# Twelve modulation weight blocks split four and eight, and relative-bias tables read from a skewed copy

## The chip, the cores and the metric

The kernel runs on one core of a Trainium2 chip. The metric is device time in microseconds (us) of one execution. A core has five engines that run their own instruction streams and meet through semaphores: TensorE (PE, with weight loads shown as PEld), VectorE (DVE), ScalarE (ACT), GpSimd (POOL) and SyncE (SP). SP issues the large weight loads, POOL the small and indirect ones. In this profile TensorE's granted clock is given as a share of its higher level: 1.0 is 2.4 GHz, 0.5 is 1.2 GHz.

## The reference

Two blocks of two layers each work on a sequence of 512 tokens of width 1024. The change touches only the first block, which for each layer does this:

```python
mod = c_act @ w_ada[l] + b_ada[l]                 # 1024 x 6144 weights, one row of input
sh1, sc1, g1, sh2, sc2, g2 = jnp.split(mod, 6, axis=-1)
h = modulate(rms_norm(x, norm1_g[l]), sh1, sc1)   # needs sh1, sc1 alone
y = token_mixer(h, ...)                           # gated linear attention and differential attention
x = x + g1[:, None, :] * y                        # needs g1
h = modulate(rms_norm(x, norm2_g[l]), sh2, sc2)   # needs sh2, sc2
y = hier_moe(h, ...)
x = x + g2[:, None, :] * y                        # needs g2
```

In the differential attention a bias is added to the scores of 4 heads. It depends on key position minus query position alone: `bucket = t5_bucket(kpos - qpos)`, `bias = rel_bias[bucket]`, 32 buckets by 4 heads. Each head makes two softmaxes p0 and p1 and uses `p0 - lam * p1` on the values.

## The kernel before, in words

Activations are held transposed: 8 tiles of 128 features by 512 tokens. Weights pass through a ring of six slots (`ring`, 2 MB each); a block is 1024 x 512 numbers of float32. The list `blocks_a` gives the blocks in the order in which SP loads them, each with its slot and the last ticket that reads it. SP walks this list in order: for each block it waits until the reader before it in that slot is done, then issues the load (line 569). `order_a` lists the tickets: each is one output of TensorE in one of the eight PSUM banks, in the order in which TensorE makes them. The consumer (`"V"` for DVE, `"A"` for ACT) frees the bank.

Modulation. `w_ada` of a layer is twelve blocks, named `("ada", j)`. For each, TensorE does 32 matmuls of 128 columns (8 row groups by 4 column groups, two records each in the trace) into one bank. DVE adds the twelve results one after another into `T[:, 0]` (lines 1414 and 1417). After the twelfth, TensorE turns that tile (`("adt",)`, line 935), DVE adds the bias into `mod` (line 1421) and makes the scales `s1` of both norms. `mod_ready` then lets ACT scale and shift the first norm's output (line 1935), after which the first projection, `("lr",)`, can start. Blocks 0 to 5 take slots 0 to 5, blocks 6 to 11 the same slots again. Blocks 0 to 3 hold sh1 and sc1; blocks 4 and 5 g1; 6 to 9 sh2 and sc2; 10 and 11 g2.

The first norm runs beside it: ACT squares x (line 1926), TensorE sums the squares, DVE and ACT take the root and its reciprocal (lines 1400, 1930, 1402), and DVE multiplies eight tiles (line 1409). DVE does this ahead of all adds of the modulation.

Differential attention. A loop of 18 iterations i over 4 heads by 4 query tiles. TensorE makes two score tiles L(i) and turns the weights of step i-2, T(i-2) (line 1059). At the last query tile of a head it multiplies by the values, pv(h). DVE in iteration i waits for T(i-2), then adds the bias and takes the row maximum (line 1556), and forms the weights of step i-1 (lines 1564 to 1567). ACT takes the exponentials (line 2046) and copies T (line 1908). The bias table of a head, 128 rows by 896, lies in one of two tiles `relm`; POOL loads it (line 689) for heads 0 and 1 long before the loop and for heads 2 and 3 when the head two before is done.

Setup. POOL writes constants and loads `c`, the bucket table and the 32 x 4 bias values. TensorE makes a tile of 4 x 1024, one row per head, and DVE copies it; POOL stores it to `rel_scratch` and reads it back 128 times with a row step of one element, so that partition p holds the row moved by p. This lies in reversed partition order, and TensorE turns it round with a reversed identity (8 matmuls of 448 columns); DVE copies the result and POOL stores it to `relm_scratch`. SP starts the first weight load only after that read-back has landed (`rel_loaded`, line 518). DVE then clears two tiles and releases the first layer. POOL waits for its stores before it issues the thirteen parameter loads of the layer.

The line that makes SP wait, and the one that sets the slots:

```python
sp.wait_ge(rel_loaded, 16 * HEADS)
return [(name, last, n % RING if n < 12 else n % 3, None) for n, (name, last) in enumerate(b)]
```

Of the kernel before, what the change touches and what calls it, by code (L numbers as in the profile page):

```python
# [34 lines left out]
P = 128  # L35
# [24 lines left out]
REL_W = 896  # L60

SCRATCH = 6144

LINKS = {"A": 176, "B": 138}
# [76 lines left out]

def order_a():
    t = [(("n1",), "V")] + [(("ada", j), "V") for j in range(12)] + [(("par",), "V"), (("adt",), "V"), (("lr",), "A")]
# [30 lines left out]
    t += [(("on", h), "V") for h in range(HEADS)]  # L174
# [16 lines left out]
def blocks_a():  # L191

    b = [(("ada", j), ("ada", j)) for j in range(12)]
    b += [(("lr",), ("lr",)), (("gqk",), ("gq", 1)), (("gv",), ("gv", 3)), (("gg",), ("gg", 3)), (("dq",), ("dq", 3)),
          (("dk",), ("dk", 3)), (("dv",), ("dv", 3))]
    for j in range(2):
        b += [((w, j), (w, 4 * j + 3)) for w in ("ga", "ya", "gb", "yb")]
    b += [(("wo", 0), ("wo", 3)), (("wo", 1), ("wo", 7)), (("rt",), ("rt",))]

    return [(name, last, n % RING if n < 12 else n % 3, None) for n, (name, last) in enumerate(b)]  # L200
# [77 lines left out]
def program(nc, ctx, inp, out):  # L278
# [52 lines left out]
    rel_dram = nc.dram_tensor("rel_scratch", [HEADS, 1024], F32).ap()  # L331
    relm_dram = nc.dram_tensor("relm_scratch", [HEADS, P, REL_W], F32).ap()
# [87 lines left out]
    rel_stored, rel_loaded = sem("rel_stored"), sem("rel_loaded")  # L420
# [81 lines left out]
    def tok(t, n=1):  # L502
        return slice(t * P, (t + n) * P)
# [5 lines left out]
    def _(sp):  # L509
# [6 lines left out]
        sp.wait_ge(started, 1)  # L516

        sp.wait_ge(rel_loaded, 16 * HEADS)
# [95 lines left out]
    def _(pool):  # L614
# [6 lines left out]

        did(pool.memset(ident[:], 0.0))
# [4 lines left out]
        did(pool.memset(T[:, 1, 0:P], 0.0))  # L627
        did(pool.affine_select(out=T[:, 1, 0:P], in_=T[:, 1, 0:P], compare_op=ALU.not_equal, fill=1.0, base=-(P - 1), pattern=[[1, P]], channel_multiplier=1))
        did(pool.iota(cells[:], pattern=[[0, 2]], base=0, channel_multiplier=0))
        pool.dma_start(prow[0:KD, 0, :], inp["c"][0].rearrange("(k p) -> k p", p=P)).then_inc(setup_d, 16)  # L630
        pool.dma_start(flat(U[0:BUCKETS, 0:2]), inp["buckets"]).then_inc(setup_d, 16)
        pool.dma_start(U[0:BUCKETS, 2, 0:HEADS], inp["rel_bias"]).then_inc(setup_d, 16)
# [38 lines left out]
        pool.wait_ge(setup_v, 1)  # L671
        pool.dma_start(rel_dram, flat(U[0:HEADS, 4:6])).then_inc(rel_stored, 16)
        pool.wait_ge(rel_stored, 16)
        for h in range(HEADS):
            row = rel_dram[h:h + 1, 0:REL_W]
            src = bass.AP(tensor=row.tensor, offset=row.offset, ap=[[1, P], [1, REL_W]])
            pool.dma_start(flat(U[:, 8 + 2 * h:10 + 2 * h])[:, 0:REL_W], src).then_inc(rel_loaded, 16)
        for h in range(HEADS):
            pool.wait_ge(setup_v, 10 + h)

            pool.dma_start(relm_dram[h], flat(U[:, 16 + 2 * h:18 + 2 * h])[:, 0:REL_W]).then_inc(m_scattered[h % 2], 16)
# [9 lines left out]
        with pool.Fori(0, DEPTH) as l:  # L691
# [26 lines left out]
            for h in range(HEADS):  # L718
# [9 lines left out]
                small(relm_in[h], relm[h % 2], relm_dram[h])  # L728
# [91 lines left out]
    def _(pe):  # L820
# [20 lines left out]
        pe.wait_ge(setup_c, 6)  # L841
        pe.wait_ge(setup_d, 48)
        for c in range(2):
            last = mm(psum[0:HEADS, c, :], U[0:BUCKETS, 2, 0:HEADS], U[0:BUCKETS, c, :], True, True)
        last.then_inc(setup_p, 1)
        pe.transpose(psum[:, 2, 0:KD], prow[0:KD, 0, :], ident[0:KD, 0:KD]).then_inc(setup_p, 1)
        for j in range(8):
            if j % 2 == 0:
                pe.wait_ge(x_in[j // 2], 16)
            if j == 5:  # L850
                pe.wait_ge(setup_v, 1)
            if j == 7:
                pe.wait_ge(setup_a, 1)
            rows = flat(hT[:, 2 * (j // 2):2 * (j // 2) + 2])
            for f in range(4):
                last = pe.transpose(psum[:, (3 + j) % 8, tok(f)], rows[:, tok(4 * (j % 2) + f)], ident[:])
            last.then_inc(setup_p, 1)
        for h in range(HEADS):
            if h == 0:
                pe.wait_ge(rel_loaded, 16 * HEADS)  # L860
                pe.wait_ge(setup_v, 9)
            for c in range(2):
                last = mm(psum[:, 2 * h + c, 0:REL_W // 2], T[:, 1, 0:P], flat(U[:, 8 + 2 * h:10 + 2 * h])[:, c * REL_W // 2:(c + 1) * REL_W // 2], True, True)
            last.then_inc(setup_p, 1)
        pe.wait_ge(setup_v, 9 + HEADS)

        with pe.Fori(0, DEPTH) as l:
# [53 lines left out]
            for j in range(12):  # L921
# [6 lines left out]
                done(last)  # L928
            o = opened(("par",))
            pe.wait_ge(params_in.sem, params_in.at(l, 13 * 16))  # L930
            done(pe.transpose(o[:, 0:NPA], prow[0:NPA, 0, :], ident[0:NPA, 0:NPA]))
            o = opened(("adt",))

            pe.wait_ge(TA.by(("ada", 11)).sem, TA.freed_at(l, ("ada", 11)))
            done(pe.transpose(o[:, 0:P], T[:, 0, 0:P], ident[:]))
# [109 lines left out]
            for i in range(HEADS * NT + 2):  # L1045
# [8 lines left out]
                if i >= 2:  # L1054
# [6 lines left out]
                    if j % NT == NT - 1:  # L1061
# [6 lines left out]
                        done(last)  # L1068
            for h in range(HEADS):
                head_sumsq(("on", h), 12 + h, ones)  # L1070
# [291 lines left out]
    def _(ve):  # L1362
# [3 lines left out]
        ve.wait_ge(setup_p, 1)  # L1366
# [901 lines left out]
```

## Time and profile before

| | us |
|---|---|
| median of 3 runs | 3999.5 |
| lowest, highest | 3993.81, 3999.94 |
| profiled execution, whole | 4006.49 |
| its span on the core | 4004.8 |
| mean granted clock, of 2.4 GHz | 0.907 |

All times of rows below are of the profiled execution, counted from the start of its span. The first block takes roughly the first 2400 us: two layers, each with projections, attention and a mixture of experts. Layer 0 begins near 40 us and layer 1 near 1275 us. A row of the timeline gives a start, a duration over which equal instructions are merged, the engine, the line, the tiles, and in brackets the engine's idle time before it with what ended that idle time.

### The profile page before, as it was taken

The page shows a single profiled execution, that of the slowest core. Times are in us where ns is not written, and L with a number is a line of the kernel's source. Part 1 is how long each engine was busy: PE and PEld are TensorE (multiplying, and loading weights), DVE is VectorE, ACT ScalarE, POOL GpSimd, SP SyncE. Part 2 cuts the span into 40 slices and gives each one's busy share as a digit, 9 for nine tenths or more (in the row PEclk, how much of TensorE's full clock was granted, in tenths as well). Part 3 has the DMA queues.
Part 4 walks back from the last instruction along what each step waited for, and adds up shares of the span by engine and source line. Part 5 has one row for each costly group of instructions (what it writes and reads, how often), then busy time and mean ns, then how long its engine had stood idle before and what let it go on. Part 6 is the DMA issues. An engine that isn't in the chain of part 4 may idle for free. (4 is left out here: it accounts for less than half of the span.)

```text
span 4004.8 us, 41122 instructions
## 1 busy us (share of the span) xinstructions
PE 3338.8 (83%) x14329; PEld 1956.9 (49%) x14329; DVE 1182.0 (30%) x2139; ACT 858.7 (21%) x1253; POOL 671.3 (17%) x367
## 2 busy tenths in 40 slices
PE   5796798788884796698788786788799988879999
PEld 3573364433332574364433332553488447338854
DVE  2356402211112347511211110363333015433310
ACT  0523211111111423311111111222232022323300
POOL 2311010111111221010111111300234021013300
PEclk7897898899997897799799999888899999889999
DMA  8311023799997421023699999210132322012222
GB/s 300 120 52 41 11 90 122 312 409 409 409 406 288 162 73 36 5 95 128 236 397 408 410 409 364 73 43 1 63 99 65 90 87 84 1 42 85 92 65 64
DMA packets 287753, 665.18 MB, mean 166 GB/s; under 512 B 20282, under 2 KB 110704, under 8 KB 287600
## 3 DMA queue, kind: packets, MB, share of 16 engines
q1 hardware_dynamic: 269632, 623.43, 41.8%
q0 software_dynamic: 17968, 39.73, 2.8%
q8 instruction: 93, 1.52, 0.2%
q14 instruction: 60, 0.49, 0.0%
HBM read 655.47 MB, written 25.44 MB: 170 GB/s over the span
## 5 line engine op out<-in xcount | busy, mean ns | idle before, releaser
L822 PE MATMUL psum<-s_parts 128*128 128x512 f32 (+3 forms) x3392 | 830.3, 398 | 112.3 <-ACT s_parts L1908 96.6
L822 PE MATMUL psum<-s_ring,s_units 128*64 128x512 f32 x3168 | 746.2, 621 | 128.7 <-DMA s_ring<-in_w_expert_in 89.9
L822 PEld LDWEIGHTS psum<-s_parts 128*128 128x128 f32 (+1 forms) x3392 | 637.6, 194 | 277.0 <-issue 99.9
L822 PEld LDWEIGHTS psum<-s_ring,s_units 128*64 128x64 f32 x3168 | 250.7, 142 | 580.8 <-issue 450.9
L822 PE MATMUL psum<-s_units,s_ring 128*128 128x512 f32 x1216 | 524.0, 593 | 3.3 <-DVE s_units L1581 3.3
L822 PE MATMUL psum<-s_units 128*128 (+9 forms) x1532 | 406.0, 450 | 128.1 <-ACT s_units L1908 52.5
L801 POOL TENSOR_TENSOR s_parts<-s_ring,s_parts 128x4096 fp32r<-128x4096 f32 x30 | 270.1, 9008 | 996.5 <-ACT s_parts L1908 996.5
L822 PEld LDWEIGHTS psum<-s_units,s_ring 128*128 128x128 f32 x1216 | 231.2, 190 | 290.5 <-issue 289.7
L822 PE MATMUL psum<-s_h_low,s_parts 128*128 128x512 f32 (+1 forms) x1440 | 355.9, 389 | 0.0
L822 PEld LDWEIGHTS psum<-s_units 64*128 64x128 f32 (+3 forms) x1532 | 206.7, 206 | 258.2 <-issue 198.2
L822 PEld LDWEIGHTS psum<-s_h_low,s_parts 128*128 128x128 f32 (+1 forms) x1440 | 269.1, 187 | 57.5
L711 POOL TENSOR_TENSOR s_parts<-s_ring,s_parts 128x4096 fp32r<-128x4096 f32 (+1 forms) x22 | 180.5, 8208 | 674.8 <-ACT s_parts L1908 674.8
L1697 DVE TENSOR_SCALAR s_put_at<-psum,s_half_row 128x1 int32<-128x1 f32 x66 | 14.4, 218 | 712.6 <-DMA ys_scratch<-s_units,s_put_at 712.6
L1908 ACT ACTIVATE s_parts<-s_ring 128x4096 fp32r<-128x4096 f32 (+1 forms) x52 | 181.3, 3494 | 196.5 <-DMA s_ring<-in_w_in 196.5
L1908 ACT ACTIVATE s_units<-psum 128x512 f32<-128x512 f32 x242 | 138.8, 591 | 272.9 <-PE psum L822 229.0
L752 POOL DMA_INDIRECT s_units<-h_scratch,s_take_at x66 | 81.8, 1240 | 595.1 <-DVE s_take_at L1692 468.7
L1892 DVE SCALAR_TENSOR_TENSOR s_units<-psum,s_par,s_units 128x511 f32<-128x511 f32 x88 | 66.0, 750 | 303.8 <-ACT s_units L2228 303.8
L2228 ACT ACTIVATE s_units<-psum,s_par 128x512 f32<-128x512 f32 x88 | 60.6, 689 | 338.2 <-PE psum L822 338.2
L1402 DVE RECIPROCAL s_temps<-s_temps 128x512 f32<-128x512 f32 x36 | 120.7, 3353 | 25.1 <-ACT s_temps L1930 25.1
L2105 ACT ACTIVATE s_units<-psum,s_gsl 128x512 f32<-128x512 f32 x66 | 45.4, 687 | 368.8 <-PE psum L822 368.8
L761 POOL DMA_INDIRECT ys_scratch<-s_units,s_put_at x66 | 66.8, 1012 | 327.0 <-ACT s_units L2105 289.5
L822 PE MATMUL psum<-s_hT,s_ring 128*128 128x512 f32 x256 | 110.4, 593 | 1.7 <-ACT s_hT L1908 1.7
(313 smaller groups left out, 2425.2 us busy)
## 6 DMA issues: line engine op xcount, KB each, us to landing
s_ring<-in_w_expert_in SPq DMA_DIRECT2D x132, 2048.0 KB, 23.7
s_ring<-in_w_expert_out SPq DMA_DIRECT2D x66, 2048.0 KB, 24.8
s_ring<-in_w_in SPq DMA_DIRECT2D x28, 2048.0 KB, 7.9
s_ring<-in_w_ada SPq DMA_DIRECT2D x24, 2048.0 KB, 19.7
s_ring<-in_ffn_w_up SPq DMA_DIRECT2D x44, 1024.0 KB, 6.7
s_ring<-in_ffn_w_down SPq DMA_DIRECT2D x16, 1408.0 KB, 7.7
s_ring<-in_w_out SPq DMA_DIRECT2D x8, 2048.0 KB, 7.8
s_units<-ys_scratch POOLq DMA_DIRECT2D x16, 512.0 KB, 6.3
```

Source lines behind the costliest of these rows:

```text
L711: pool.tensor_tensor(parts[:, s, 0:size], ring[:, s, 0:size], parts[:, 4 + n % 2, 0:size].bitcast(F32), ALU.subtract).then_inc(weights_low ...
L752: pool.indirect_dma_start(out=xs[u % 2], out_offset=None, in_=h2_dram[:, :], in_offset=bass.IndirectOffsetOnAxis(ap=take_at[:, u % 2, 0:1] ...
L761: pool.indirect_dma_start(out=ys_dram[:, :], out_offset=bass.IndirectOffsetOnAxis(ap=put_at[:, u, 0:1], axis=0), in_=ys[u], in_offset=None ...
L801: pool.tensor_tensor(parts[:, RB.slot(SPLIT_B[n]), :], raw, parts[:, 4 + n % 2, :].bitcast(F32), ALU.subtract).then_inc(weights_low.sem, w ...
L822: return pe.matmul(o, lhsT=lhsT, rhs=rhs, start=start, stop=stop)
L1402: link(ve.reciprocal(T[:, 2, :], T[:, 3, :]))
L1697: ve.tensor_scalar(put_at[:, u % 2, :], psum[:, 7, 1:2], 2.0, half_row[:, 0:1], ALU.mult, ALU.add).then_inc(m_put_written.sem, m_put_writt ...
L1892: link(ve.scalar_tensor_tensor(out=up_t[:, b, 1:SEQ], in0=o[:, 0:SEQ - 1], scalar=w[0], in1=up_t[:, b, 1:SEQ], op0=ALU.mult, op1=ALU.add))
L1908: return ae.activation(o, i, ACT.Copy) if scale is None else ae.activation(o, i, ACT.Copy, scale=scale)
L2105: ae.activation(ys[u], psum[:, 5 + u, :], ACT.Copy, scale=gsl[:, u:u + 1]).then_inc(m_ys_made.sem, m_ys_made.more())
L2228: ae.activation(up_t[:, n % 4, :], o, ACT.Copy, scale=par[:, col:col + 1]).then_inc(up_centre.sem, up_centre.more())
```

## The change

It has four parts.

1. `blocks_a` and `order_a`: only `("ada", 0)` to `("ada", 3)` stand ahead of the first norm's end, in slots 3, 4, 5 and 2. `("lr",)` and `("gqk",)` follow in slots 0 and 1 with no earlier reader in this layer. `("ada", 4)` to `("ada", 11)` all take slot 2, each after the one before; block 4 follows `("dk",)` there.
2. The attention loop: in iterations i = 1, 3, ..., 15 TensorE makes one such block behind T(i-2) and pv, and DVE adds it behind the weights of step i-1. A second turn, `("adt", 1)`, and the second half of `mod` and `s1` follow the loop. ACT waits for that turn before it squares the heads.
3. The bias tables: DVE spreads the 32 x 4 values to 32 x 512; TensorE makes the row of each head in all 128 partitions at once (8 matmuls of 512 columns), ACT copies, POOL stores 128 x 1024. The layers read it back with a row step of 1023 elements, so that partition p begins p elements earlier. The read-back, the reversed identity and the second store are gone.
4. Setup order: POOL issues its three loads first, SP waits for a zeroed cell alone (`cells_zero`), TensorE turns x first.

```diff
-    b = [(("ada", j), ("ada", j)) for j in range(12)]
+    b = [(("ada", j), ("ada", j), s) for j, s in enumerate((3, 4, 5, 2))]
+    b += [(("lr",), ("lr",), 0), (("gqk",), ("gq", 1), 1), (("gv",), ("gv", 3), 2), (("gg",), ("gg", 3), 0), (("dq",), ("dq", 3), 1),
+          (("dk",), ("dk", 3), 2), (("dv",), ("dv", 3), 0), (("ga", 0), ("ga", 3), 1), (("ada", 4), ("ada", 4), 2), (("gb", 0), ("gb", 3), 0)]
+    b += [(("ada", j), ("ada", j), 2) for j in range(5, 12)]
...
+def late_ada(i):
+
+    return 4 + i // 2 if i % 2 == 1 and i < 16 else None
...
-        sp.wait_ge(started, 1)
-
-        sp.wait_ge(rel_loaded, 16 * HEADS)
+        sp.wait_ge(cells_zero, 1)
...
-            src = bass.AP(tensor=row.tensor, offset=row.offset, ap=[[1, P], [1, REL_W]])
-            pool.dma_start(flat(U[:, 8 + 2 * h:10 + 2 * h])[:, 0:REL_W], src).then_inc(rel_loaded, 16)
...
+            pool.wait_ge(setup_a, 2 + h)
+            pool.dma_start(rel_dram[h], flat(U[:, 8 + 2 * h:10 + 2 * h])).then_inc(m_scattered[h % 2], 16)
...
-                small(relm_in[h], relm[h % 2], relm_dram[h])
+                row = rel_dram[h, 0:1, P - 1:P - 1 + REL_W]
+                small(relm_in[h], relm[h % 2], bass.AP(tensor=row.tensor, offset=row.offset, ap=[[REL_N - 1, P], [1, REL_W]]))
...
+            for j in range(4):
+                ada(j)
...
+                if late_ada(i):
+                    ada(late_ada(i))
+            turn_ada(1, 11)
...
+                if late_ada(i):
+                    add_ada(late_ada(i))
+            modulation(1, 4, 12)
```

SP's queue at the start of a layer, before. `in_w_ada` with 128x8x512 is one modulation block, `in_w_in` with 128x8x32 is `("lr",)`.

```order
L569 DMA s_ring<-in_w_ada 128x8x512
L569 ISA
L569 DMA s_ring<-in_w_ada 128x8x512
L569 ISA
L569 DMA s_ring<-in_w_ada 128x8x512
```

And after, the same place:

```order
L575 DMA s_ring<-in_w_ada 128x8x512
L575 ISA
L575 DMA s_ring<-in_w_in 128x8x32
L575 REGISTER_ALU
L575 DMA s_ring<-in_w_in 128x8x512
```

After the fourth modulation block (the first row) the two first projections' weights now follow at once; before, eight more modulation blocks stood between.

TensorE in the attention loop, before. `s_ident,s_units` 128x128 x4 is T, `s_units` 128x512 a score matmul L.

```order
L822 MATMUL psum<-s_units 128x512
L877 REGISTER_ALU
L1059 MATMUL psum<-s_ident,s_units 128x128 x4
L877 REGISTER_ALU
L822 MATMUL psum<-s_units 128x512
```

And after, at iteration 3; `s_ring,s_cact` is one modulation block's last matmuls.

```order
L819 MATMUL psum<-s_units 128x512
L867 REGISTER_ALU
L1055 MATMUL psum<-s_ident,s_units 128x128 x4
L867 REGISTER_ALU
L913 REGISTER_ALU
L819 MATMUL psum<-s_ring,s_cact 32x128 x32
L867 REGISTER_ALU
L819 MATMUL psum<-s_units 128x512
```

In odd iterations a modulation block now stands between a turn T and the next two score matmuls.

## Rows read from the trace of the kernel before

**Rows 1.** Timeline, start of the program (start us, us, engine, line, operation, idle before)

```profile
0.90 1.82 SPq L515 DMA_DIRECT2D s_hT<-in_x  x4
...
16.13 3.85 DVE L1370 COPY s_xT<-psum 128x512 f32<-128x512 f32 x6 [0.16 <-PE psum L856]
...
29.77 8.23 PE L822 MATMUL psum<-s_units,s_temps 128*128 128x448 f32 x16 [11.16 <-DMA s_units<-rel_scratch]
...
31.11 59.70 SPq L569 DMA_DIRECT2D s_ring<-in_w_ada  x12
...
39.38 1.03 DVE L1380 MEMSET s_units<- 128x512 f32 x2 [0.25 <-DVE s_units L1374]
40.56 4.26 ACT L1926 ACTIVATE s_hT<-s_xT 128x512 f32<-128x512 f32 x8 [27.00 <-DVE s_sc L1382]
42.48 9.55 PE L822 MATMUL psum<-s_hT,s_ones 128*128 128x512 f32 x16 [4.48 <-ACT s_hT L1926]
```

**Rows 2.** Timeline, modulation of layer 0 on PE and DVE

```profile
61.66 0.28 DVE L1414 COPY s_temps<-psum 128x128 f32<-128x128 f32 x1
...
94.70 3.64 PE L822 MATMUL psum<-s_ring,s_cact 128*32 128x128 f32 x64 [1.70 <-DMA s_ring<-in_w_ada]
...
100.17 1.96 PE L822 MATMUL psum<-s_ring,s_cact 128*32 128x128 f32 x64 [1.83 <-DMA s_ring<-in_w_ada]
...
109.99 0.21 DVE L1421 TENSOR_TENSOR s_mod<-psum,s_par 128x48 f32<-128x48 f32 x1 [0.28 <-PE psum L935]
```

**Rows 3.** Busy time by stretch; last three: granted clock, DMA share, GB/s

```profile
31.11:109.99 78.88, 50.25 (x801) 35.87 (x799) 17.89 (x30) 7.46 (x11) 8.75 (x17) 0.77 1.03 376
341.86:457.33 115.47, 64.15 (x163) 26.82 (x164) 60.56 (x144) 42.52 (x92) 19.76 (x6) 0.66 0.04 11
```

**Rows 4.** DMA issues of the page: KB each, median us from issue to landing

```profile
s_ring<-in_w_in SPq DMA_DIRECT2D x28, 2048.0 KB, 7.9
s_ring<-in_w_ada SPq DMA_DIRECT2D x24, 2048.0 KB, 19.7
```

**Rows 5.** Small DMA issues, whole program, the same columns

```profile
s_units<-relm_scratch POOLq DMA_DIRECT2D x8, 448.0 KB, 3.6
s_units<-rel_scratch POOLq DMA_DIRECT2D x4, 448.0 KB, 5.2
relm_scratch<-s_units POOLq DMA_DIRECT2D x4, 448.0 KB, 6.8
```

**Rows 6.** Timeline, layer 1: results loaded by POOL, first norm, modulation

```profile
1237.31 2.19 POOL L689 DMA_DIRECT2D s_units<-ys_scratch  x4 [5.45 <-issue]
1248.23 1.23 DVE L1767 TENSOR_TENSOR s_units<-s_units 128x1024 f32<-128x1024 f32 x1 [22.89 <-DMA s_units<-ys_scratch]
...
1284.61 7.62 PE L822 MATMUL psum<-s_ring,s_cact 128*32 128x128 f32 x270
...
1294.32 0.29 DVE L1414 COPY s_temps<-psum 128x128 f32<-128x128 f32 x1
1294.64 0.94 DVE L1417 TENSOR_TENSOR s_temps<-psum,s_temps 128x128 f32<-128x128 f32 x3
...
1327.37 0.21 DVE L1421 TENSOR_TENSOR s_mod<-psum,s_par 128x48 f32<-128x48 f32 x1 [0.41 <-PE psum L935]
```

**Rows 7.** Timeline, PE in the attention of layer 0: T(0), then pv(0) to L(8)

```profile
361.00 1.09 PE L1059 MATMUL psum<-s_ident,s_units 128*128 128x128 f32 x4 [13.54 <-DVE s_units L1567]
...
380.00 7.38 PE L822 MATMUL psum<-s_units 128*128 128x512 f32 x12 [3.88 <-ACT s_units L1908]
387.30 0.66 PE L1059 MATMUL psum<-s_ident,s_units 128*128 128x128 f32 x4
387.89 1.13 PE L822 MATMUL psum<-s_units 64*128 64x512 f32 x4
391.55 0.63 PE L1059 MATMUL psum<-s_ident,s_units 128*128 128x128 f32 x4 [2.53 <-DVE s_units L1567]
392.11 2.08 PE L822 MATMUL psum<-s_units 64*128 64x512 f32 x4
```

## What I predict, and why

> **What bounds the kernel now.** I read the busy time by stretch first, then the timeline of each stretch that the change touches. In the stretch from the first modulation load to the end of the modulation of layer 0, the DMA engines are busy all the time at 376 GB/s, while PE works 50 of 79 us and DVE 18 [rows 3]. So there the twelve loads of 2 MB end last: SP issues the first at 31.1 us, and `mod` is written at 110.0 us, 6.6 us per load [rows 1, 2]. That late start has its own reason: PE is idle for 11.2 us until the read-back of the bias row lands, and SP's first load waits for the same read-back [rows 1]. In the attention it is the other way round: DMA has 0.04 of its time filled at 11 GB/s, PE works 64 of 115 us and DVE 61, and the clock is granted at 0.66 on average, between its two levels [rows 3]. There a chain PE, DVE, ACT, DVE, PE of one step sets the time. The change takes loads from the first place to the second.
>
> **Start of layer 0.** I rebuild the chain to ACT's first square, which stands at 40.6 us. x is issued at 0.9 us [rows 1]; the first of its copies by DVE can come near 6.6 us, an estimate (issue, a landing of about 5 us as for the 448 KB bias row read [rows 5], and PE's turns). Six copies take 3.85 us back to back but with their gaps the eight need 0.85 each, 6.8 us in all, so they end at 13.4 us. The new broadcast of the bias values is one more DVE operation of that size: 14.1 us. Then eight matmuls of 512 columns: the eight of 448 took 8.23 us [rows 1], times 512/448 is 9.4, so 23.5 us. DVE's clears, 1.2 us from their start to the first square [rows 1], and ACT's last copy run side by side: squares at 24.9 us. Gain 15.6 us; bounds 11 (x lands late, or the eight matmuls all run at the lower clock) and 18 (all at the higher).
>
> Squares to `mod`: the sum of squares ends at 42.48 + 9.55 = 52.0 us, `mod` is written 58.0 us later [rows 1, 2]. After the change four blocks are needed, and their loads are issued near 3 us; with x they are 10 MB, at 376 GB/s done near 30 us, long before PE wants them. Then the first norm ends last: from the end of the sum to the first add is 61.66 - 52.03 = 9.6 us, which PE's four blocks (4 x 1.96 = 7.8 us [rows 2]) fit under. Three adds take 0.94 us [rows 6], so four 1.25; turn and bias 0.5. That is 11.4 us for 58.0, a gain of 46.6. What would be late next is POOL's thirteen parameter loads: POOL now waits for four stores of 512 KB issued until about 25 us. The last store lands 6.8 us after its issue [rows 5], thirteen issues of 0.55 us (2.19 for four [rows 6]) are 7.1, and a landing under load 5.2 [rows 5]: 25.5 + 6.8 + 7.1 + 5.2 = 44.6 us, and `mod` wants them at about 47. So they are hidden by some 2 us; if stores are slowed by the loads beside them, up to 10 us of the gain goes. Both pieces together: 62, bounds 48 and 66.
>
> **Start of layer 1.** Six blocks are already loaded when PE reaches them, so the gain is smaller. PE starts at 1284.6, `mod` is written at 1327.4, that is 42.8 us; DVE's first add comes at 1294.3 [rows 6]. With four adds and the turn, `mod` would be written at 1294.3 + 1.25 + 0.5 = 1296.0: a gain of 31.4, bounds 28 and 32. Ahead of this stands a place where loads could hurt: the results of the experts are issued at 1237.3 and DVE waits 22.9 us in all until 1248.2 for them [rows 6], sharing the DMA engines with the weights. Before, SP prefetched slots 0, 1, 2 first, which come free first; now slot 3 is first, so loads start later, but there are 10 MB for 12. I take a loss of 1 us, bounds -2 and 5.
>
> **Attention, per layer.** Eight blocks enter PE's stream. A block costs 1.96 us when PE's clock is up and 3.64 when it is not [rows 2]. DVE's add of 0.3 us falls where DVE waits for T, and costs nothing; if that cover is gone, 8 x 0.3 = 2.4 us.
> - i = 1: PE is idle 13.5 us before T(0) [rows 7]. Nothing.
> - i = 5, 9, 13 (behind pv): PE's pv and L run until 387.3 and T(4) follows without idle time [rows 7], so PE ends last, and each block is paid in full. PE has been busy, so 1.96: 5.9 us.
> - i = 3: the block is loaded. PE must fit T, block and two L (1.09 + 1.96 to 3.64 + 2.08) into a step of 4.25 (387.30 to 391.55) to about 4.7 us: 1 us, bounds 0 and 2.
> - i = 7, 11, 15: all late blocks share slot 2, so a load is issued when the block before is done. Count from e, the end of the block behind pv. Its successor lands at e + 0.25 + 7.9 = e + 8.15 [rows 4]. PE does L (1.1), T(4) (0.7), L, and T(5) 4.25 after T(4): it is free at e + 6.1, waits 2, computes to e + 11.1 (3.0, near the middle of 1.96 and 3.64, since it waited), makes L(8) by e + 12.5. T(6) would have come at e + 10. So 2.5 us each, 7.5 us; bounds 1.6 and 4.
> The sum is 14.4 us; bounds 7 (a busier PE keeps its clock up, so T takes 0.66 for 1.09 and L 1.13 for 2.08 [rows 7]) and 25 (every block at 3.64, late landing). I take 14, for two layers 28. The second turn and second half of `mod` behind the loop are under 1 us beside ACT's copy and squares.
>
> **Bias tables.** The skewed read comes in place of a straight one, 3.6 us to landing; the old read with a row step of one element took 5.2 [rows 5]. These are the bounds. It is issued two heads, over 24 us, ahead of its use, so nothing in either case. The projections behind the attention find ya's weights late only if the load after block 11 is not there when the first gate is done, 25 us later: nothing.
>
> **Sum.** -62 - 31.4 + 28 + 1 = -64.4 us. Against the profiled 4006.5 that is 3942; the median of the runs is 7 us below that execution, so 3999.5 - 64.5 = 3935.
>
> **Rivals.**
> (a) The attention takes the blocks almost free, since PE's clock is up: 7 a layer. 3935 - 14 = 3921. For it: the granted clock there is 0.66, so there is room to gain [rows 3]. Against: behind pv PE ends last already [rows 7].
> (b) The blocks are dear: each behind a wait for its load and at the lower clock. Costs of 25 a layer, 3935 + 22 = 3957. For it: 3.64 us at 94.7 us. Against: 1.96 at 100.2 us behind a wait of the same length [rows 2]. The Trainium skill, in "TensorE: Matmul & The Clock Gate", section "Loop structure matters more than you think", calls a DMA wait ahead of every matmul the bad loop nest, whose matmuls run cold; by that rule all eight blocks would cost the longer time, and the trace agrees in part of its blocks.
> (c) Parameters or stores take the place of the modulation loads at the start: 12 less there, 3947.
> (d) Slower than before: the chain through slot 2. The gains are 94 us; seven gaps in each layer, fourteen in all, would have to cost 6.7 us each. That happens if a load lands 4 us or more later than 7.9 in every gap. At 19.7 us, the landing in the full queue [rows 4], each gap costs 2.5 + 11.8 or less by the slack of pv steps, about 11: 3935 + 140 = 4075. Against it: the queue is empty there [rows 3].
> (e) The change does not do what it says, the first norm waits for something else and the gain is spent: within 0.2%, 3999.
>
> **How the numbers follow.** Chances: forecast (3925 to 3946) 0.55, (a) 0.17, (b) 0.18, (c) 0.07, (d) 0.02, (e) 0.01. Ends of terms added, 66 + 32 - 14 + 2 = 86 and 48 + 28 - 50 - 5 = 21, give 3914 and 3978; all bad ends at once are unlikely, and I stop at 3960, which takes in (a), (b) and (c). A change of 0.2%, 8 us, is about what this measurement tells from none. Faster by more: 0.97; within: 0.01; slower: 0.02.
>
> **What would show it.** Right: first square of ACT near 25 us; SP's first modulation load near 3 us; `mod` near 48 us; in layer 1 `mod` 11 to 12 us after PE's sum; the step behind pv longer by 2 us, PE waiting about 2 us for `in_w_ada` in iterations 7, 11 and 15; the whole attention about 14 us longer. Wrong: a PE wait for the parameters ahead of `("par",)`, DVE waiting longer than 23 us for the experts' results, blocks of 3.6 us throughout the attention, or an attention that grows by over 25 us.

## The result, and the profile after

| | before | after |
|---|---|---|
| median of the runs made side by side, us | 3996.65 | 3928.2 |
| lowest, highest | 3991.98, 3999.94 | 3926.26, 3930.32 |
| ratio, with its 95% interval | | 0.983 (0.9813 to 0.9847) |
| profiled execution, whole | 4006.49 | 3928.03 |
| its span | 4004.8 | 3926.4 |
| mean granted clock | 0.907 | 0.917 |

The change takes 68 us away. The forecast was 3935.0 in a range of 3914 to 3960; the time is 7 us below the forecast. I read the trace of after in the order of the program and compare each milestone with its row of before.

**Start.** The timeline of the first 46 us of the changed kernel (start us, us, engine, line, operation, idle time before it and what ended that):

```profile
4.71 11.54 SPq L575 DMA_DIRECT2D s_ring<-in_w_ada  x4
...
12.05 10.91 PE L819 MATMUL psum<-s_units 32*128 32x512 f32 x16 [1.51 <-DVE s_units L1370]
...
24.39 4.26 ACT L1936 ACTIVATE s_hT<-s_xT 128x512 f32<-128x512 f32 x8 [0.38 <-DVE s_sc L1378]
25.52 8.79 PE L819 MATMUL psum<-s_hT,s_ones 128*128 128x512 f32 x16 [2.56 <-ACT s_hT L1936]
...
33.50 0.56 POOL L685 DMA_DIRECT2D s_prow<-in_b_ada  x1 [8.66 <-issue]
34.24 7.20 PE L819 MATMUL psum<-s_ring,s_cact 128*32 128x128 f32 x256
...
43.94 0.29 DVE L1410 COPY s_temps<-psum 128x128 f32<-128x128 f32 x1
44.27 0.94 DVE L1413 TENSOR_TENSOR s_temps<-psum,s_temps 128x128 f32<-128x128 f32 x3
44.73 0.28 PE L930 MATMUL psum<-s_ident,s_prow 72*128 72x72 f32 x1 [3.29 <-DMA s_lamv<-in_diff_lambda]
45.26 0.33 PE L924 MATMUL psum<-s_ident,s_temps 128*128 128x128 f32 x1 [0.25 <-DVE s_temps L1413]
45.63 0.17 DVE L1418 TENSOR_TENSOR s_mod<-psum,s_par 128x16 f32<-128x16 f32 x1 [0.28 <-PE psum L924]
```

SP's first load stands at 4.7 us, where I had put it near 3; nothing waited for it. ACT's first square stands at 24.4 us, for 40.6 before [rows 1]; PE's four blocks (7.2 us, without a wait for a load) lie under the first norm; `mod` is written at 45.6 us for 110.0 [rows 2]. Only the row at 44.73 shows a wait that was not there before: PE waited 3.29 us for the last of POOL's parameters. It cost nothing yet: PE had turned them by 45.0 us (44.73 + 0.28) and then stood idle for 0.25 us more, until DVE's last add had ended at 45.2 us. Parameters later by more than this 0.25 us would have moved `mod`.

**Layer 1.** The timeline at its start, in the changed kernel; it answers to [rows 6].

```profile
1196.45 1.23 DVE L1774 TENSOR_TENSOR s_units<-s_units 128x1024 f32<-128x1024 f32 x1 [21.48 <-DMA s_units<-ys_scratch]
...
1232.41 7.20 PE L819 MATMUL psum<-s_ring,s_cact 128*32 128x128 f32 x256
...
1243.81 0.17 DVE L1418 TENSOR_TENSOR s_mod<-psum,s_par 128x16 f32<-128x16 f32 x1 [0.28 <-PE psum L924]
```

From PE's first block to `mod` it is now 11.4 us (1232.4 to 1243.8), for 42.8. DVE's wait for the experts' results is 21.48 us for 22.89.

**Attention.** Busy time by stretch: start and end, length, busy us (and instructions) of PE, PE's weight loads, DVE, ACT and POOL, then granted clock, DMA share and GB/s. From the last matmul ahead of the attention to the first matmul of `("ga", 0)`, layers 0 and 1, first the kernel before:

```profile
341.86:466.06 124.20, 67.13 (x169) 27.69 (x169) 67.74 (x149) 45.36 (x96) 19.76 (x6) 0.68 0.04 10
1560.21:1684.83 124.62, 68.42 (x169) 28.30 (x169) 67.74 (x149) 45.37 (x96) 19.62 (x6) 0.65 0.03 10
```

and the changed one, with the whole second block of the network, which no line of the change touches, as its third row:

```profile
277.15:417.10 139.95, 82.80 (x682) 43.78 (x682) 70.28 (x159) 45.38 (x96) 19.64 (x6) 0.74 0.36 123
1475.26:1615.11 139.85, 82.93 (x681) 43.87 (x682) 70.25 (x159) 45.39 (x96) 19.64 (x6) 0.74 0.36 122
2449.02:3926.40 1477.38, 1352.63 (x4828) 851.88 (x4828) 494.67 (x738) 345.31 (x488) 276.32 (x57) 0.94 0.20 63
```

PE is busy for 15.7 us more in the attention (82.80 for 67.13) and the attention is 15.75 us longer. That the two are so close is chance, and does not show that nothing of the moved work is hidden. In layer 0 the eight blocks take 22.4 us of PE's time (2.18, 3.44, three of 1.95 and three of 3.64), PE's other work takes 6.7 us less than before at a granted clock of 0.74 for 0.68, and PE waits 7.3 us for loads. The second block took 8.2 us longer in the profiled execution of before:

```profile
2519.18:4004.80 1485.62, 1358.64 (x4828) 856.39 (x4828) 495.25 (x738) 345.09 (x488) 276.43 (x58) 0.94 0.20 63
```

The same matmuls, and 6 us more of busy PE. In the nine profiled executions of the experiments below this block takes 1477.7 to 1481.9 us, so that of before is the longest of the eleven. I therefore take 8.2 of the 78.4 us between the two profiled spans as no part of the change, and the 70.2 that are left answer to the 68.5 between the medians. The balance:

| stretch | before | after | difference | predicted |
|---|---|---|---|---|
| start to `mod`, layer 0 | 109.99 | 45.63 | -64.4 | -62 |
| attention, layer 0 | 124.20 | 139.95 | +15.75 | +14 |
| layer 1: PE's first block to `mod` | 42.8 | 11.4 | -31.4 | -31.4 |
| attention, layer 1 | 124.62 | 139.85 | +15.2 | +14 |
| all other stretches of the first block | | | -5.4 | +1 |
| first block in all (start of the second) | 2519.18 | 2449.02 | -70.2 | -64.4 |

**PE in the attention.** The timeline of layer 0 in the changed kernel, from pv(0) on; `s_ring,s_cact` is a modulation block, 128x128 x4 a turn T. The first are pv(0), block 6, L, T(4), L, T(5), and then block 7.

```profile
315.46 5.46 PE L819 MATMUL psum<-s_units 128*128 128x512 f32 x8 [3.88 <-ACT s_units L1915]
320.84 1.95 PE L819 MATMUL psum<-s_ring,s_cact 128*32 128x128 f32 x64
322.73 1.13 PE L819 MATMUL psum<-s_units 64*128 64x512 f32 x4
323.79 0.66 PE L1055 MATMUL psum<-s_ident,s_units 128*128 128x128 f32 x4
324.38 1.13 PE L819 MATMUL psum<-s_units 64*128 64x512 f32 x4
328.04 0.63 PE L1055 MATMUL psum<-s_ident,s_units 128*128 128x128 f32 x4 [2.53 <-DVE s_units L1570]
...
331.08 3.64 PE L819 MATMUL psum<-s_ring,s_cact 128*32 128x128 f32 x64 [2.42 <-DMA s_ring<-in_w_ada]
334.66 1.82 PE L819 MATMUL psum<-s_units 64*128 64x512 f32 x4
336.41 0.66 PE L1055 MATMUL psum<-s_ident,s_units 128*128 128x128 f32 x4
```

The block behind pv is in the way with all of its 1.95 us: T(4) follows L with no idle time. Block 7 waits 2.42 us for its load and then takes 3.64 us. The profile's page puts the load's landing, as the median of all 24 modulation loads, at

```profile
s_ring<-in_w_ada SPq DMA_DIRECT2D x24, 2048.0 KB, 8.1
```

us, where it stood at 19.7 in the full queue [rows 4]. Laid against the turns of before, step by step, the attention of layer 0 is longer by this (T(n) to T(n+1), us):

| step | before | after | longer by | predicted |
|---|---|---|---|---|
| i = 3 (T(1) to T(2)) | 4.68 | 5.44 | 0.8 | 1 |
| i = 5, 9, 13 (behind pv) | 12.27, 11.29, 11.03 | 12.83, 13.34, 13.51 | 0.6, 2.0, 2.5 | 1.96 each |
| i = 7, 11, 15 (second load of a pair) | 4.22, 4.65, 4.62 | 8.37, 8.54, 6.82 | 4.1, 3.9, 2.2 | 2.5 each |

These seven steps are 16.1 us longer together, and all the others 0.3 us shorter.

### The profile page after: what moved, and what is told of

Read it like the earlier page. It is cut to its first block and busy times, and to the rows that moved or that the text cites. A ratio compares the mean times of both kernels' runs of the same rounds, so it can differ in the third digit from the quotient of the medians.

```text
span 3926.4 us, 41122 instructions
## 1 busy us (share of the span) xinstructions
PE 3308.7 (84%) x14327; PEld 1938.3 (49%) x14327; DVE 1194.5 (30%) x2137; ACT 863.4 (22%) x1257; POOL 669.9 (17%) x360
## 3 DMA queue, kind: packets, MB, share of 16 engines
q1 hardware_dynamic: 269632, 623.43, 42.8%
## 5 line engine op out<-in xcount | busy, mean ns | idle before, releaser
L1915 ACT ACTIVATE s_units<-psum 128x512 f32<-128x512 f32 (+1 forms) x246 | 143.2, 598 | 285.7 <-PE psum L819 236.9
## 6 DMA issues: line engine op xcount, KB each, us to landing
s_ring<-in_w_expert_out SPq DMA_DIRECT2D x66, 2048.0 KB, 24.9
```

The lines of the kernel that those rows point to most:

```text
L1915: return ae.activation(o, i, ACT.Copy) if scale is None else ae.activation(o, i, ACT.Copy, scale=scale)
```

## Experiments

Two questions stood after this. Do the parts of the change carry what the sum gives them? And is the cost of the attention the waits for the loads, the matmuls themselves, or the place where the blocks stand?

### The split of the modulation alone

The setup, SP's first wait and the bias tables are as before; the blocks are split four and eight.

```diff
-        sp.wait_ge(cells_zero, 1)
+        sp.wait_ge(started, 1)
+        sp.wait_ge(rel_loaded, 16 * HEADS)
...
-                small(relm_in[h], relm[h % 2], bass.AP(tensor=row.tensor, offset=row.offset, ap=[[REL_N - 1, P], [1, REL_W]]))
+                small(relm_in[h], relm[h % 2], relm_dram[h])
```

> The split of the modulation alone (parts 1 and 2 of the change); bias tables and setup order stay as before. My theory: the first load still starts at 31 us, but four loads then end under the first norm, which ends last. Layer 0: sum of squares ends at 52.0 us, mod 11.4 us later at 63.4, a gain of 46.6; layer 1 gains 31.4; the attentions lose 31 together (15.5 each, as the changed kernel's trace shows). About 47 us faster than before, near 3950. Rival 1, the two halves of the change add up independently: then this one would give 68.5 less the gain of the setup half alone (its run beside this one). Rival 2, the loads still end last in layer 0: mod at 60 to 65 only if the fourth load has landed; if not, mod near 70 and 3957.

Measured: 3953.2 us, ratio 0.9889 (0.9872 to 0.9905). PE's fourth block and `mod`, on its timeline:

```profile
61.80 3.03 PE L830 MATMUL psum<-s_ring,s_cact 128*32 128x128 f32 x64 [3.25 <-DMA s_ring<-in_w_ada]
...
65.83 0.17 DVE L1439 TENSOR_TENSOR s_mod<-psum,s_par 128x16 f32<-128x16 f32 x1 [0.41 <-PE psum L942]
```

The split is worth 44.2 us at the start of layer 0 even without the early loads. The fourth load, not the norm, then ends last: PE waits 3.25 us for it, and `mod` comes 2.4 us later than the 63.4 that I had expected. The attention of layer 0 took 141.6 us, 1.7 us longer than in the changed kernel; I have not followed up why.

### The setup and the bias tables alone

All twelve blocks stay in one piece; setup order, SP's early loads and the skewed read are as changed.

```diff
-    b = [(("ada", j), ("ada", j), s) for j, s in enumerate((3, 4, 5, 2))]
+    b = [(("ada", j), ("ada", j)) for j in range(12)]
...
-            for j in range(4):
-                ada(j)
+            for j in range(12):
```

> The other half alone: skewed bias tables and setup order (parts 3 and 4), with twelve blocks ahead of the first norm's end as before. My theory: loads start near 4.7 us, but x, twelve blocks and the four stores of 512 KB are 28 MB, at 376 GB/s 74 us, so mod is written near 83 us: a gain of 27 us, near 3970, loads still ending last all the way. Sum of both halves alone: 47 + 27 = 74, more than the 68.5 of the whole, since the halves shorten the same stretch. Rival: the halves add up exactly, so this one gains 21, 3975. Rival 2: the read with the row step of 1023 elements costs in the attention; then that stretch is longer than 124 us here.

Measured: 3968.53 us, ratio 0.9931 (0.9915 to 0.9948). Its timeline at the last block and `mod`, and its attention of layer 0 as a stretch:

```profile
81.18 3.47 PE L811 MATMUL psum<-s_ring,s_cact 128*32 128x128 f32 x64 [3.50 <-DMA s_ring<-in_w_ada]
...
85.52 0.21 DVE L1400 TENSOR_TENSOR s_mod<-psum,s_par 128x48 f32<-128x48 f32 x1 [0.28 <-PE psum L917]
```
```profile
314.98:438.20 123.22, 64.71 (x168) 27.07 (x169) 67.66 (x149) 45.38 (x96) 19.61 (x6) 0.69 0.04 11
```

The first four blocks are there when PE comes; from the fifth on PE waits for the loads, to the last of them, so the earlier start (first load at 4.7 us for 31.1) passes to `mod` almost whole: 24.5 of 26.4 us. The attention reads its bias tables through the skewed step here and takes 123.2 us for 124.2: no cost of the skewed read shows. The two halves give 44.6 and 29.3 us, 73.9 together, while the whole gives 68.5. The intervals of these three numbers are 6 to 7 us wide to either side, so the medians alone don't tell 73.9 from 68.5. The stretch from the start to `mod` does: it is shorter by 44.2 and 24.5 us, 68.7 together, and by 64.4 in the whole. Both halves shorten that one stretch, and once the norm ends last there the second of them buys less.

### Loads of 32 KB in the place of 2 MB

Blocks 5 to 11 load 64 numbers of each partition. Most of their weights are left out, so the second part of the modulation is computed from what lies in the slot; every matmul is made.

```diff
-                    sp.dma_start(slot_view(s, k, n), src).then_inc(weights_in_a[s], 16)
+                    if name[0] == "ada" and name[1] >= 5:
+                        sp.dma_start(slot_view(s, k, n)[:, 0:1, 0:64], src[:, 0:1, 0:64]).then_inc(weights_in_a[s], 16)
+                    else:
+                        sp.dma_start(slot_view(s, k, n), src).then_inc(weights_in_a[s], 16)
```

> The changed kernel with the loads of blocks 5 to 11 cut to 32 KB each, so that these blocks are multiplied with what lies in the slot (this part of the modulation is computed from wrong weights). All matmuls, adds and their places stay. My theory: the step with a load wait costs 4.1, 4.1 and 2.2 us in each layer (T(5) to T(6) took 8.4 us and not 4.25), and that goes with the load: attention 129 to 130 us for 140, 21 us less in all, near 3907. Rival, the blocks' compute is the cost and not their loads: the attention stays over 136 us, 3920 or more.

Measured: 3909.04 us, ratio 0.9785 (0.9769 to 0.9802). The stretch of layer 0, and on PE the step of block 7:

```profile
277.63:407.67 130.04, 77.55 (x682) 40.53 (x682) 70.01 (x159) 45.37 (x96) 19.64 (x6) 0.78 0.07 22
```
```profile
329.12 3.04 PE L822 MATMUL psum<-s_ring,s_cact 128*32 128x128 f32 x64
...
333.69 0.66 PE L1058 MATMUL psum<-s_ident,s_units 128*128 128x128 f32 x4
```

Block 7 no longer waits, and T(5) to T(6) is 5.12 us (328.57 to 333.69) for 8.37. Of the 15.75 us that the attention grew, 9.9 are the waits for the loads and what follows from them, and 5.8 (130.04 against 124.20) go with the matmuls. Step by step the 5.8 are not three times 1.95: the steps behind pv are 0.6, 2.0 and 3.1 us longer than before, those of i = 3 and 7 are 0.8 and 0.9 us longer, and the others give 1.5 us back.

### Another place for the blocks

The late blocks stand where PE was idle before: at i = 1 and ahead of T(0) at i = 2, ahead of pv at i = 5, 9, 13, and one iteration later at 6, 10, 14.

```diff
-    return 4 + i // 2 if i % 2 == 1 and i < 16 else None
+    return {1: 4, 2: 5, 5: 6, 6: 7, 9: 8, 10: 9, 13: 10, 14: 11}.get(i)
...
```

> The changed kernel with the same eight late blocks at other places of the loop: in i = 1 as now, in i = 2 ahead of T(0), in i = 5, 9, 13 ahead of pv instead of behind it, in i = 6, 10, 14 instead of 7, 11, 15. Nothing else differs. My theory: the blocks cost where PE ends last (behind pv, 2.0 us each) and where a load has only two short steps (about 4 us each). Ahead of pv PE waits 3.9 us for ACT, and from there to the turn of the next iteration are over 12 us, longer than a load of 8.2 us and its block. So the attention returns from 140 us to 124 to 126 us in each layer, about 29 us less than the changed kernel, near 3899. Rival, the blocks' own time on PE is what costs wherever they stand: no more than 12 us less, 3916 or slower.

Measured: 3898.23 us, ratio 0.9754 (0.9738 to 0.9771).

```profile
276.31:399.26 122.95, 77.75 (x682) 42.53 (x682) 70.24 (x159) 45.39 (x96) 19.66 (x6) 0.79 0.40 141
```
```profile
309.90 3.64 PE L823 MATMUL psum<-s_ring,s_cact 128*32 128x128 f32 x64
313.85 5.24 PE L823 MATMUL psum<-s_units 128*128 128x512 f32 x12 [0.31 <-ACT s_units L1923]
...
347.16 1.95 PE L823 MATMUL psum<-s_ring,s_cact 128*32 128x128 f32 x64 [2.12 <-DMA s_ring<-in_w_ada]
```

PE does all eight blocks (77.75 us of work, for 77.55 in the kernel with small loads) in 122.95 us, 1.2 us under the stretch of before. Ahead of pv the block fills the wait for ACT's copy, of which 0.31 us is left of 3.88 [rows 7].

### Only the three blocks of the pv steps moved

The changed kernel, with the block between T and pv at i = 5, 9, 13; the odd iterations stay.

```diff
                 if (i - 2) % NT == NT - 1:
+                    if late_ada(i):
+                        ada(late_ada(i))
...
-                if late_ada(i):
+                if late_ada(i) and not (i > 2 and i % NT == 1):
```

> The changed kernel with one reordering alone: in i = 5, 9, 13 the block stands between T and pv instead of behind pv. i = 1, 3, 7, 11, 15 stay. My theory: the 2.0 us behind pv go (6 us a layer), and the next load starts 5 to 7 us earlier, so that the waits in i = 7, 11, 15 vanish; but from those odd places to the next place ahead of pv are only two short steps, so a load wait of 1 to 3 us now stands ahead of pv, of which the 3.9 us that PE waits there for ACT hide most. Attention 126 to 130 us for 140, near 3906. Rival, the load wait only moves and is paid in full there: attention 134 us or more, 3916.

Measured: 3897.81 us, ratio 0.9751 (0.9733 to 0.9769): three blocks moved by one instruction group give 30 us against the changed kernel.

```profile
278.64:404.01 125.37, 79.17 (x681) 43.92 (x682) 69.97 (x159) 45.37 (x96) 19.62 (x6) 0.77 0.40 137
```
```profile
313.27 0.63 PE L1057 MATMUL psum<-s_ident,s_units 128*128 128x128 f32 x4 [2.54 <-DVE s_units L1574]
...
316.83 3.64 PE L821 MATMUL psum<-s_ring,s_cact 128*32 128x128 f32 x64 [2.94 <-DMA s_ring<-in_w_ada]
320.41 5.68 PE L821 MATMUL psum<-s_units 128*128 128x512 f32 x12
...
330.26 0.63 PE L1057 MATMUL psum<-s_ident,s_units 128*128 128x128 f32 x4 [2.53 <-DVE s_units L1574]
330.82 1.96 PE L821 MATMUL psum<-s_ring,s_cact 128*32 128x128 f32 x64
...
334.47 0.63 PE L1057 MATMUL psum<-s_ident,s_units 128*128 128x128 f32 x4 [0.64 <-DVE s_units L1574]
```

It came out below what I had expected, and the reason is in these rows. Block 6 now has to wait 2.94 us for its load, but this wait and the block, 6.6 us, lie for 3.9 us under the wait for ACT's copy, which PE had in any case. And from the end of block 6 (320.4 us), when the load of block 7 can start, to the point where PE wants it (330.8) there are 10.4 us, for 5.9 in the changed kernel (322.7 to 328.6), and the landing takes 8.1. So it is there when PE comes, block 7 takes 1.96 us, and T(5) to T(6) is 4.21 us, the 4.22 of before. Both costs of this first pair shrink with one move. In the later pairs the second block finds its load there too, but runs at 2.9 and 3.0 us.

### Both together

The block ahead of pv and the small loads (the second part of the modulation is again computed from what lies in the slot).

> The block ahead of pv in i = 5, 9, 13 and also the loads of blocks 5 to 11 cut to 32 KB (that part of the modulation computed from wrong weights). My theory: with neither a load wait nor work behind pv, the blocks' matmuls are free, and a busier PE holds its clock up: attention 122 to 125 us, not above the 124.2 of the kernel before. Rival, the blocks' time on PE costs something in the short steps too (4.25 us each, into which T, block and L must fit): 128 us or more.

Measured in one execution: 3890.57 us, and the attention of layer 0

```profile
277.17:399.32 122.15, 80.10 (x681) 44.05 (x682) 69.86 (x159) 45.38 (x96) 19.64 (x6) 0.78 0.07 23
```

In that order the matmuls of eight blocks, 13 us of PE's busy time, cost nothing (122.15 for 124.20), and the waits for the loads in the kernel before this one cost 3 us a layer (125.37 for 122.15).

### What ends last at the start

The bias row of head 0 is made once and used for all four heads (heads 1 to 3 get the wrong bias), so that two matmuls stand there in the place of eight.

```diff
-            for c in range(2):
-                last = mm(psum[:, 2 * h + c, :], U[0:BUCKETS, 3, tok(h)], U[0:BUCKETS, c, :], True, True)
-            last.then_inc(setup_p, 1)
+            if h == 0:
+                for c in range(2):
+                    last = mm(psum[:, c, :], U[0:BUCKETS, 3, tok(h)], U[0:BUCKETS, c, :], True, True)
+                last.then_inc(setup_p, HEADS)
```

> The changed kernel with the bias row of the first head made once and copied for all four heads (heads 1 to 3 get a wrong bias), so 2 matmuls of 512 columns for 8 in the setup. My theory: those matmuls held up the first norm by 8 us, but POOL's start flag at 19 us and then its parameter loads, which landed 0.5 us ahead of need, end last in their place: squares at 20 us for 24.4, mod near 41 to 42 us for 45.6. Rival, only the matmuls count: mod at 37.5 us.

Measured in one execution: 3927.83 us, no gain over 3928.2. The square came as expected, `mod` did not. Its timeline on POOL, ACT, PE and DVE:

```profile
19.18 2.21 POOL L677 DMA_DIRECT2D rel_scratch<-s_units  x4
20.39 4.26 ACT L1937 ACTIVATE s_hT<-s_xT 128x512 f32<-128x512 f32 x8 [2.60 <-DVE s_sc L1379]
...
33.30 0.56 POOL L685 DMA_DIRECT2D s_prow<-in_b_ada  x1 [11.91 <-issue]
...
46.23 0.38 PE L931 MATMUL psum<-s_ident,s_prow 72*128 72x72 f32 x1 [6.58 <-DMA s_lamv<-in_diff_lambda]
...
47.01 0.17 DVE L1419 TENSOR_TENSOR s_mod<-psum,s_par 128x16 f32<-128x16 f32 x1
```

POOL issued its last store by 21.4 us, 3.4 us earlier than in the changed kernel, and yet stood idle until 33.3, as there until 33.5. The landings of the four stores, one by one, say why: they are complete at 25.8, 27.7, 29.7 and 31.6 us here and at 25.8, 27.8, 29.7 and 31.7 us in the changed kernel. They land about 2 us apart; the last one here, issued at 20.9 us, takes 10.7 us, where that of the changed kernel, issued at 24.3 us, takes 7.4. In both kernels POOL's first parameter load follows 1.7 to 1.8 us after the last landing. The parameters come behind that and take the norm's place at once. To see whether POOL's wait for the stores does this or the landing of the small loads themselves, I moved that wait from ahead of the parameters to ahead of the first bias-table load of a layer:

```diff
-        for u in range(2):
-            pool.wait_ge(m_scattered[u], 32)
...
+            for u in range(2):
+                pool.wait_ge(m_scattered[u], 32)
             for h in range(HEADS):
                 if h == 2:
                     low_part(7)
```

> As the run with one bias row (heads 1 to 3 with the wrong bias), and POOL waits for its four stores only ahead of the first bias-table load of a layer, so the thirteen parameter loads are issued right behind the stores. Theory, that POOL's wait for the stores holds the parameters: they are issued at 21.5 to 29 us, have landed by 36, PE waits for nothing ahead of the turn, and mod is written 21.2 us after the first square as in the changed kernel, at 41 to 42 us instead of 47.0; the time is 5 us below 3927.8, about 3923. Rival, that the small loads themselves land late as long as the weight loads fill the DMA engines: PE still waits for lamv until 41 us or later, and mod stays at 43 to 47.

Measured in one execution: 3922.95 us.

```profile
22.52 0.56 POOL L683 DMA_DIRECT2D s_prow<-in_b_ada  x1 [1.11 <-issue]
...
40.90 0.28 PE L931 MATMUL psum<-s_ident,s_prow 72*128 72x72 f32 x1
...
42.95 0.17 DVE L1419 TENSOR_TENSOR s_mod<-psum,s_par 128x16 f32<-128x16 f32 x1 [0.28 <-PE psum L925]
```

The parameters are issued from 22.5 us and PE waits for none of them, though the first of them takes 9.4 us to land for 5.3; `mod` comes 4.1 us earlier and the time is 4.9 us lower, each from one execution. `mod` is 1 us behind the 42 that I gave as the latest. So it was the wait for the stores that held the parameters. The same move in the complete kernel with the block ahead of pv, without the cut of the bias rows:

> The complete kernel with the block ahead of pv, and POOL's wait for the stores moved in the same way. Theory (store wait holds the parameters, but with only 0.5 us to lose, the first norm ends last right behind): mod at 45.0 to 45.7, no wait of PE for lamv, and the time stays at that of the kernel with the block ahead of pv, 3897.8, less 0 to 1 us. Rival (small loads land late among the weight loads): parameters land after 45 us and mod moves to 46 to 48, time 3898 to 3900.

Measured: 3897.59 us, ratio 0.9761 (0.9745 to 0.9778); for the same kernel without the move it was 3897.81. The parameters were issued from 28.36 us and held nobody up. `mod` stood at 47.83 us, outside what I had expected, and not for the parameters' sake: the eight matmuls of the bias rows took 12.78 us here, so that the first square stood at 26.80, and from square to `mod` it was 21.0 us for 21.2. As long as the norm ends last, the move is worth nothing.

## Why the prediction was right, and where it was off

**Layer 0, predicted -62, measured -64.4.** The chain is the one that the sum followed, though two of its first terms were off and cancelled. The copies of x ended at 11.7 us, not 13.4; the eight matmuls began at 12.05 for 14.1, but took 10.91 us, not 9.4; the first square came at 24.39 for 24.9. From the end of the sum of squares (34.31 us) `mod` is 11.3 us away for 11.4. The rest of the difference is the sum of squares itself, which I had carried over at its old length: it ended 11.5 us behind the first square of before [rows 1] and now 9.9 us behind.

**The parameters, predicted to be hidden by some 2 us, were hidden by 0.25.** They landed at 44.7 us for 44.6, but that the landing came out so close is luck: the last store was issued at 24.3 and not 25.5 us, landed in 7.4 and not 6.8 us, POOL then let 1.8 us pass that the sum did not have, and the last parameter took 4.5 us for the 5.2 that I had taken for a landing under load. (That 5.2 belongs to reads at 22 us, before the first weight load [rows 1, 5], and so is none.) The 1.8 us could have been seen in the trace of before, where the last store, landed 6.8 us after its issue at 46.2 us, has the same distance to the first parameter load:

```profile
39.42 0.54 POOL L681 DMA_DIRECT2D relm_scratch<-s_units  x1 [0.96 <-DVE s_units L1374]
...
48.02 0.53 POOL L689 DMA_DIRECT2D s_prow<-in_b_ada  x1 [8.06 <-issue]
```

`mod` wanted the parameters earlier than I had it, since the chain of the norm was shorter. Rival (c) did not come true, by a quarter of a microsecond. The cut bias row shows that the parameters are the next bound: as long as POOL waits for the stores, a quicker start buys nothing.

**Layer 1, predicted -31.4, measured -31.4.** Three adds behind the first one, the turn and the bias were all that was left, at the durations of before. The loads beside the experts' results cost nothing where I took 1 us (DVE's wait is 21.48 us for 22.89); from the experts' last matmul to the sum of squares it was 45.1 us for 46.5.

**The attention, predicted +14, measured +15.75 and +15.2.** The mechanism was right: nothing at i = 1, a full block behind pv in two steps of three, a wait for the load at 7, 11 and 15. The small loads confirm the two parts: 5.8 us go with the matmuls (predicted 5.9 behind pv and 1 for i = 3), the rest with the chain through slot 2. That term was mis-sized, 10.2 us for 7.5. Its waits were 2.42, 2.33 and 2.59 us for 2, its blocks took 3.64 us for the 3.0 that I had put between the two rows of before, L(8) behind it 1.8 for 1.4, and T(6) of before came some 0.4 us earlier than I had reckoned. Against it the first pv step cost only 0.6 us: the granted clock rose from 0.68 to 0.74, and pv(0) and L took 5.46 + 1.13 us for 7.38 before [rows 7]. That is rival (a)'s argument. It holds for one of the three pv steps and for three short ones, T(2) to T(3), T(6) to T(7) and T(12) to T(13), each 0.3 to 0.4 us shorter than before.

**Rival (b)** was half right in what it saw. The blocks behind a wait for their load did run at the lower level, 3.64 us in all three pairs of layer 0, though the turn before that wait took the 0.63 us of the higher level. The Trainium skill ("TensorE: Matmul & The Clock Gate", section "Loop structure matters more than you think") calls a load's wait ahead of matmuls the cold case, and there the trace agrees; behind pv the same block took 1.95 us, and the attention as a whole was 16 us longer and not 25. But a wait for a load does not by itself bring the lower level: with the blocks at another place the one at 347.16 stands behind a wait of 2.12 us and took 1.95 us, and with small loads block 7 took 3.04 us behind no wait at all. What (b) missed is that more of the time lay in when the load could start than in the matmuls: 9.9 of the 15.75 us went with the small loads.

**The remaining 5.4 us** that the first block is shorter by I can place only in part: the projections and the mixture of experts of both layers have less in them here and there, 0.3 us ahead of the first attention, 3.2 from its end to the norm of layer 1 (1.4 of those at the experts' results), 1.4 ahead of the second attention and 0.4 behind it. Their instructions are unchanged, and an execution differs from another by this much (8.2 us in the second block), so I take them for that and not for the change; this is argued and not shown.

**The conversion** from the profiled execution to the median was right in kind: the profiled execution of before lay 7 us above the median, and its second block was 8.2 us longer than that of the changed kernel.

**The whole.** That the forecast came within 7 us is in part luck. Of the parts that the sum has, the start of layer 0 gave 2.4 us more and the two attentions cost 3.0 us more than predicted, which nearly cancel; what is left lies in the other stretches of the first block, predicted +1 and measured -5.4.

## What to carry to other kernels

Work that is moved into a loop should stand in a gap where its engine waits in any case, ahead of the instruction that ends that wait and not behind it; the same three blocks moved from behind pv to ahead of it took about 15 us off each layer's attention. When moved loads share one buffer, the time from the end of one use to the next use must hold the landing (8.1 us here), so a block that is done earlier pays twice. And a landing time is not yet the time at which the next thing is issued: POOL let 1.8 us pass between the two. When a start-up chain is shortened, look up what lies close behind it (here, 0.25 us behind, a wait for stores that nobody needed yet) before anything more is taken from it.

## What the runs showed that I had not expected

The last of the four stores of 512 KB at the start was complete at 31.6 to 31.7 us whether POOL had issued it at 20.9 or at 24.3 us. Weight loads alone don't explain this: in the kernel before, the four stores of 448 KB had loads of 2 MB beside them too (the DMA engines at 395 GB/s from 34.5 to 46.2 us, for 406 from 19.2 to 31.7 in the changed kernel), and each landed in 6.7 to 6.8 us. There they were issued 1.5 to 1.9 us apart, while with one bias row they come 0.55 us apart and land 2 us apart. I take it that stores so close queue behind each other; no run changes their distance alone. The small parameter loads next to the same traffic were in time when issued at 22.5 to 29.8 us.

The eight matmuls of 512 columns that spread the bias took 10.91 us in one execution and 12.78 in another of a kernel with the same start. With them, and a start that was 0.5 us later, the first square moved by 2.4 us. That is more than the whole slack of the parameters (0.25 us), so a gain of a microsecond at the start can't be read from one profile.
